# A plain weight unit split in two parts, in a fused two-block transformer kernel

## The chip, the cores and the metric

The kernel runs on one core of one Trainium2 chip. The metric is the device time of one execution in microseconds; the median of three runs of the kernel before is 2380.12 us (2380.11 to 2380.45). Every time below is from those runs or from one profiled execution.

## The reference, cut to what matters

Two transformer blocks follow each other on x of 1024 tokens by 1024 channels. The first has an HGRN2 mixer, the second a mixer of convolution and retention; both end in a squared-ReLU MLP with 4096 hidden channels, all float32:

```python
def _squared_relu_mlp(h, w1, w2):
    a = jax.nn.relu(h @ w1)
    return (a * a) @ w2

def sq_relu_mlp(u, w_up, w_down):
    hdn = jax.nn.relu(u @ w_up)
    return (hdn * hdn) @ w_down

x = x + _squared_relu_mlp(_rmsnorm(x, norm_mlp[layer]), mlp_w1[layer], mlp_w2[layer])   # block 1
h = h + sq_relu_mlp(rms_norm(h, norm2_g), w_up, w_down)                                 # block 2
```

The change touches only the product `h @ w1` (and `u @ w_up`) of the two MLPs, and there only the order in which weights are prepared.

## The kernel before, in words

**Products.** Each float32 operand is used as a high part (a cast to `fp32r`) and a low part (the float32 value minus the high part). A product of a 128x128 weight tile with 512 tokens is three matmuls: high by high, high weight by low operand, low weight by high operand (in `upper`, L905, L906 and L907; in `wino`, L820, L821 and L822).

**Weights.** They arrive as units of 128 x 8 x 128 floats (512 KB) in `w_raw`, which has two slots. Even units use slot 0 and odd ones slot 1. SyncE loads the units in order (`load_units`, L398, the load is L395) and waits for `w_split` before a slot is loaded again: unit n is loaded once units 0 to n - 2 are split.

**The MLP.** Its up product makes two hidden tiles of 128 channels at a time, an up pair, of which there are 16 in each MLP. An up pair takes two units. The first, in slot 0, holds the first 512 input channels and is used in a Winograd form: seven products of quarter size (A11, S1, A12, S2, S4, S3, A22) against prepared sums of the operand. GpSimd, ScalarE and VectorE make its parts together (`split_pair`, L478, with `weight_sums` on VectorE and `weight_highs` on ScalarE). The second, in slot 1, is the plain unit: input channels 512 to 1023 for both hidden tiles. Its slices 0 to 3 belong to the first hidden tile and slices 4 to 7 to the second. GpSimd alone splits it, in `split_unit` (L445): one cast of all 1024 columns (L450), and behind a wait for it four subtractions of 256 columns (L454), the last of which raises `w_split`.

**TensorE's order in an up pair** (`up_pair`, L911): A11, S1, A12, S2, S4, each of 6 matmuls, then the first plain block `upper(b_w, 0, 0)` with 12 matmuls, S3, the second plain block `upper(b_z, 1, 1)`, A22, and two more plain blocks. The first argument after the bank chooses the hidden tile, and so the half of the plain unit: 0 reads slices 0 to 3, 1 reads slices 4 to 7. Ahead of the first plain block stands

```python
pe.wait_ge(w_split, at(g, 8, u + 2))
```

which is true once the whole plain unit is split, and a second wait for `w_split` at u + 1 stands ahead of A22. Results of an up pair are taken from PSUM by VectorE (`finish_up`, L1546) and ScalarE (`copy`, L2234). A22 waits for `up_taken`, which VectorE raises once it has read what S3 left in the same bank; S3 waits for ScalarE's third copy of the pair.

**Groups.** Each MLP runs two up pairs, six groups, and two more up pairs. A group is an up pair in the near banks (b_w in `prod_ps`), four down pairs (`pairs`, L857), and an up pair in the far banks (b_w in `side_ps`). The first five groups are a hardware loop. A near pair follows directly on a far pair. In the near pair of a group VectorE also builds sums and low parts of hidden activations for the down pairs (`near_phase`, L1600: five instructions of 1024 columns at L1536 and L1532). In the near pair behind the last group it does not; the hidden tiles left are used in plain form.

**Who does what on GpSimd.** `split_mlp` (L497) goes through the units in order: for an up pair `split_pair` and then `split_unit`, which waits until the unit has landed and until TensorE is done with the previous unit in slot 1.

Of the kernel before, what the change touches and what calls it, by code (L numbers as in the profile page):

```python
# [37 lines left out]
ALU = mybir.AluOpType  # L38
ACT = mybir.ActivationFunctionType
F32 = mybir.dt.float32  # L40
# [15 lines left out]
WINO_GROUPS = 6  # L56
# [10 lines left out]
MLP_PLAIN_DOWN = WINO + (WINO + PAIRS) * WINO_GROUPS + 4  # L67
# [5 lines left out]
UP_PAIRS = FF // (2 * P)  # L73
MLP_PAIRS = UP_PAIRS + PAIRS * WINO_GROUPS
# [83 lines left out]
def at(g, step, first):  # L158

    return g * step + first  # L160


def build(nc, stream, x_t, gains, conv_w, lower_bound, head_rows, head_scalars, rope, ident_in, ones_in, masks_in, out_t):
    with ExitStack() as ctx:
# [15 lines left out]
        def sem(name):  # L180
            return ctx.enter_context(nc.semaphore(name))
# [8 lines left out]
        w_raw = place("w_raw", [P, 2, KT, P])  # L190
        w_hi = place("w_hi", [P, 2, KT, P], F32R)
        at_w_lo = room(8 * KB)
        w_lo = place("w_lo", [P, 2, KT, P], F32R, at=at_w_lo)
# [90 lines left out]
        w_landed = [sem("w_landed0"), sem("w_landed1")]  # L284
# [5 lines left out]
        high_begun = sem("high_begun")  # L290
        high_made = sem("high_made")
        w_split = sem("w_split")
        tiles_used = sem("tiles_used")
        prod = sem("prod")
# [9 lines left out]
        w_sum = sem("w_sum")  # L304
        w_high = sem("w_high")
        w_parts = sem("w_parts")
        down_prod = sem("down_prod")
        down_taken = sem("down_taken")
        up_prod = sem("up_prod")
# [134 lines left out]
        def _(pool):  # L444
            def split_unit(u, slot):  # L445
                pool.wait_ge(w_landed[slot], (u - slot) * 8 + 16)
                if not (isinstance(u, int) and u < 2):
                    pool.wait_ge(prod, u * 2 - 2)
                pool.sem_inc(high_begun, 1)
                nc.gpsimd.tensor_copy(w_hi[:, slot], w_raw[:, slot]).then_inc(high_made, 1)  # L450
                pool.wait_ge(high_made, u + 1)
                for part in range(4):
                    ks = slice(part * KT // 4, (part + 1) * KT // 4)
                    low = nc.gpsimd.tensor_tensor(w_lo[:, slot, ks], w_raw[:, slot, ks],  # L454
                                                  w_hi[:, slot, ks].bitcast(F32), ALU.subtract)
                low.then_inc(w_split, 1)
# [21 lines left out]
            def split_pair(u, slot, q):  # L478
# [15 lines left out]
                low(a22_lo[slot][:], w_raw[:, slot, 6:8], more_hi[slot][:, 4:6], 4).then_inc(w_split, 1)  # L494
                pool.sem_inc(high_made, 1)

            def split_mlp(u0, index):  # L497

                def up_pair(u, q):
                    split_pair(u, 0, q)  # L500
                    split_unit(u + 1, 1)

                def group(g, q):
                    up_pair(at(g, 8, u0 + 4), at(g, 6, q + 2))
                    for p in range(PAIRS):
                        split_pair(at(g, 8, u0 + 6 + p), p % 2, at(g, 6, q + 3 + p))
                    up_pair(at(g, 8, u0 + 10), at(g, 6, q + 7))

                q = index * MLP_PAIRS
                up_pair(u0, q)  # L510
                up_pair(u0 + 2, q + 1)
                with pool.Fori(0, WINO_GROUPS - 1) as g:
                    group(g, q)
                group(WINO_GROUPS - 1, q)
                up_pair(u0 + MLP_PLAIN_DOWN - 4, q + MLP_PAIRS - 2)
                up_pair(u0 + MLP_PLAIN_DOWN - 2, q + MLP_PAIRS - 1)

            for u in range(2):
                for part in range(4):
                    ks = slice(part * KT // 4, (part + 1) * KT // 4)  # L520
# [5 lines left out]
                    else:  # L526
                        high.then_inc(high_made, 1)
                        pool.wait_ge(high_made, u + 1)
                    low = nc.gpsimd.tensor_tensor(w_lo[:, u, ks], w_raw[:, u, ks], w_hi[:, u, ks].bitcast(F32),
                                                  ALU.subtract)  # L530
# [15 lines left out]
        def _(pe):  # L546
# [281 lines left out]
            def mlp(u0, index, before, h_before, t_norm, count, roots, left=0):  # L828


                first_group, first_up, first_pair = index * WINO_GROUPS, index * UP_PAIRS, index * MLP_PAIRS

                def parts(g, q, part):
                    pe.wait_ge(w_parts, at(g, 24, 4 * (first_pair + q) + part))

                def free(g, p, name):
                    pe.wait_ge(down_taken, at(g, PAIR_PRODUCTS, first_group * PAIR_PRODUCTS + pair_index(p, name)))
# [55 lines left out]
                def upper(into, i, half, first, start, mid=None):  # L893

                    act = slice(half * HALF, (half + 1) * HALF)
                    for kk in range(KT - X_WINO):
                        k = X_WINO + kk
                        if start:
                            pe.wait_ge(u_ready, before + 2 * k + half + 1)
                        if kk == 2 and mid is not None:  # L900
                            mid()
                        w_h, w_l = w_hi[:, 1, 4 * i + kk], w_lo[:, 1, 4 * i + kk]
                        a_h, a_l = hi[0][:, k, act], lo[0][:, k, act]
                        more = not (first and kk == 0)
                        nc.tensor.matmul(into, w_h, a_h, start=not more, stop=False, skip_group_check=not first)  # L905
                        nc.tensor.matmul(into, w_h, a_l, start=False, stop=False, skip_group_check=not first)  # L906
                        mm = nc.tensor.matmul(into, w_l, a_h, start=False, stop=kk == KT - X_WINO - 1,  # L907
                                              skip_group_check=not first)
                    return mm

                def up_pair(g, r, q, u, into, start=False, behind_down=False, hooks=(None, None, None, None), last=False):  # L911

                    b_u, b_v, b_w, b_z = into
                    u += u0
                    after_p5, after_p3, after_p7, in_last = hooks

                    def copied(n):
                        pe.wait_ge(up_copied, at(g, 8, 4 * (first_up + r) + n))

                    parts(g, q, 1)  # L920
                    if start:
                        pe.wait_ge(u_ready, before + 2 * X_WINO)
                    pe.wait_ge(evac, at(g, 16, 2 * u - 2 if start else 2 * u - 4))
                    if behind_down:
                        free(g, PAIRS - 2, "P4")
                    wino(b_u, 0, A11, x_op[B11], True).then_inc(up_prod, 1)
                    parts(g, q, 2)
                    pe.wait_ge(evac, at(g, 16, 2 * u - 2))
                    wino(b_v, 0, S1, x_op[T1], True).then_inc(up_prod, 1)
                    if after_p5 is not None:  # L930
                        after_p5()
                    if start:
                        pe.wait_ge(evac, 2 * u - 1)
                    wino(b_w, 0, A12, x_op[B21], True)
                    parts(g, q, 3)
                    copied(1)
                    wino(b_u, 0, S2, x_op[T2], False).then_inc(up_prod, 1)
                    parts(g, q, 4)
                    copied(2)
                    wino(b_v, 0, S4, x_op[B22], False)  # L940
                    if after_p3 is not None:
                        after_p3()
                    pe.wait_ge(w_split, at(g, 8, u + 2))
                    upper(b_w, 0, 0, False, start).then_inc(up_prod, 1)
                    copied(3)
                    wino(b_u, 0, S3, x_op[T3], False).then_inc(up_prod, 1)
                    if after_p7 is not None:
                        after_p7()
                    if start:
                        pe.wait_ge(evac, 2 * u)  # L950
                    upper(b_z, 1, 1, True, start).then_inc(up_prod, 1)
                    pe.wait_ge(w_split, at(g, 8, u + 1))
                    pe.wait_ge(up_taken, at(g, 2, first_up + r + 1))
                    wino(b_u, 0, A22, x_op[T4], False).then_inc(prod, 2)
                    if last:
                        upper(b_u, 1, 0, False, start).then_inc(up_prod, 1)
                        upper(b_v, 0, 1, False, start, in_last).then_inc(prod, 2)
                    else:
                        upper(b_v, 0, 1, False, start).then_inc(up_prod, 1)
                        upper(b_u, 1, 0, False, start, in_last).then_inc(prod, 2)  # L960

                def group(g):
                    up_pair(g, 2, 2, 4, near_banks, hooks=(None, None, None, lambda: first(g, 0)))
                    pairs(g)
                    up_pair(g, 3, 7, 10, far_banks, behind_down=True,
                            hooks=(lambda: fourth(g, PAIRS - 1), None, None, None))
# [10 lines left out]
                u = u0 + MLP_PLAIN_DOWN  # L977
# [109 lines left out]
            for j in range(CONV_TILES):  # L1087
                for part in range(3):
                    u = U_CONV + 3 * j + part
# [1430 lines left out]
```

## Time and profile before

| what | value |
|---|---|
| median of the timed runs | 2380.12 us |
| profiled execution | 2377.08 us |
| its span, first to last instruction | 2374.5 us |
| TensorE busy | 2331.4 us, 98% |
| VectorE busy | 1499.9 us, 63% |
| GpSimd busy | 1068.4 us, 45% |
| ScalarE busy | 724.5 us, 31% |
| mean granted TensorE clock | 0.997 of full speed |

In the rows PE is TensorE's matmul, DVE is VectorE, ACT is ScalarE, POOL is GpSimd and SP is SyncE. Matmuls overlap: each of 512 columns is listed with 0.39 us, while the next begins about 0.23 us after it. The distance between the starts of two matmuls is therefore what counts. A wait is listed under the instruction that waited, with what released it.

### The profile page before, as it was taken

How to read it: one execution, taken by the hardware profiler on the slowest of the kernel's cores; microseconds unless marked ns; L12 is line 12 of the kernel's file. 1: busy time of each engine (PE TensorE's matmuls, PEld its weight loads, DVE VectorE, ACT ScalarE, POOL GpSimd, SP SyncE). 2: the span in 40 equal slices, each digit the busy share in tenths (PEclk: the TensorE clock that was granted, in tenths of full speed). 3: DMA queues.
4: the chain of work that ended last, by engine and by line, in shares of the span. 5: the costliest groups of instructions: out<-in, count | busy, mean ns of one | idle time of the engine just before them, and what ended most of it. 6: DMA issues, size and time to landing. Idle time of an engine off the chain costs nothing.

```text
span 2374.5 us, 31836 instructions
## 1 busy us (share of the span) xinstructions
PE 2331.4 (98%) x11044; PEld 1939.2 (82%) x11044; DVE 1499.9 (63%) x2090; ACT 724.5 (31%) x1175; POOL 1068.4 (45%) x1186
## 2 busy tenths in 40 slices
PE   9999999999999999999999999999999999999998
PEld 6888888888787778778888888888877877787886
DVE  6666667756567666765566656454666676667434
ACT  4233333423433432333330002003343333323311
POOL 4322232345456555645443324453554565555432
PEclk9999999999999999999999999999999999999999
DMA  4110101031111111111111111111111111111112
GB/s 151 36 36 27 36 26 36 27 107 62 45 54 54 51 54 53 53 44 54 54 52 64 36 45 36 54 36 54 38 54 52 53 53 44 60 55 45 49 58 80
DMA packets 37526, 123.33 MB, mean 52 GB/s; under 512 B 4800, under 2 KB 5952, under 8 KB 37440
## 3 DMA queue, kind: packets, MB, share of 16 engines
q1 hardware_dynamic: 36432, 120.54, 16.0%
q10 hardware_dynamic: 1008, 1.62, 0.2%
q8 instruction: 57, 0.93, 0.2%
q14 instruction: 29, 0.24, 0.0%
HBM read 117.95 MB, written 4.19 MB: 51 GB/s over the span
## 4 chain that ended last, share of the span: by engine, by line
PE 82%; POOL 7%; issue 7%; DVE 2%; DVEq 1%; DMA 0%; SPq 0%; ACT 0%; POOLq 0%
PE prod_ps L563 13%; PE prod_ps L565 13%; PE prod_ps L564 13%; PE side_ps L822 4%; PE side_ps L821 4%; PE side_ps L820 4%; POOL w_lo L454 4%; PE prod_ps L822 4%; PE prod_ps L821 4%; PE prod_ps L820 4%; PE prod_ps L905 3%; PE prod_ps L906 3%; PE prod_ps L907 3%; PE side_ps L700 2%; PE side_ps L616 2%
## 5 line engine op out<-in xcount | busy, mean ns | idle before, releaser
L563 PE MATMUL prod_ps<-operand_hi,w_hi 128*128 128x512 f32 x1464 | 584.0, 399 | 2.9 <-DVE hgrn_v_t L1150 1.6
L565 PE MATMUL prod_ps<-operand_hi,w_lo 128*128 128x512 f32 x1464 | 572.6, 391 | 0.0
L564 PE MATMUL prod_ps<-operand_lo,w_hi 128*128 128x512 f32 x1464 | 571.4, 390 | 0.0
L454 POOL TENSOR_TENSOR w_lo<-w_raw,w_hi 128x256 fp32r<-128x256 f32 x472 | 470.5, 1027 | 9.4
L450 POOL CAST w_hi<-w_raw 128x1024 fp32r<-128x1024 f32 x118 | 125.9, 1067 | 733.8 <-PE prod_ps L565 680.2
L484 POOL TENSOR_TENSOR w_lo<-w_raw,w_hi 128x256 fp32r<-128x256 f32 x160 | 144.0, 918 | 454.6 <-ACT w_hi L2172 454.6
L563 PEld LDWEIGHTS prod_ps<-operand_hi,w_hi 128*128 128x128 f32 x1464 | 275.9, 188 | 61.1 <-issue 3.3
L565 PEld LDWEIGHTS prod_ps<-operand_hi,w_lo 128*128 128x128 f32 x1464 | 275.5, 188 | 59.1
L564 PEld LDWEIGHTS prod_ps<-operand_lo,w_hi 128*128 128x128 f32 x1464 | 276.1, 189 | 53.4
L905 PE MATMUL prod_ps<-operand_hi,w_hi 128*128 128x512 f32 x384 | 151.7, 395 | 22.5 <-POOL w_lo L454 22.5
L906 PE MATMUL prod_ps<-operand_lo,w_hi 128*128 128x512 f32 x384 | 150.5, 392 | 0.0
L907 PE MATMUL prod_ps<-operand_hi,w_lo 128*128 128x512 f32 x384 | 150.2, 391 | 0.0
L484 POOL TENSOR_TENSOR w_lo<-w_s,w_hi 128x256 fp32r<-128x256 f32 x160 | 118.1, 748 | 41.8 <-ACT w_more_hi L2176 24.6
L1540 DVE TENSOR_TENSOR x_res<-side_ps,x_res 128x512 f32<-128x512 f32 x168 | 113.1, 684 | 32.3 <-PE side_ps L822 30.4
L484 POOL TENSOR_TENSOR w_s_lo<-w_s,w_more_hi 128x256 fp32r<-128x256 f32 x160 | 129.7, 831 | 0.0
L1540 DVE TENSOR_TENSOR x_res<-prod_ps,x_res 128x512 f32<-128x512 f32 x120 | 82.4, 687 | 70.9 <-PE prod_ps L822 69.7
L1532 DVE TENSOR_TENSOR wino_lo<-wino,wino_hi 128x1024 fp32r<-128x1024 f32 x72 | 99.7, 1397 | 17.9 <-ACT wino_hi L2228 15.9
L905 PEld LDWEIGHTS prod_ps<-operand_hi,w_hi 128*128 128x128 f32 x384 | 72.5, 189 | 42.7 <-POOL w_lo L454 27.7
L1266 DVE TENSOR_TENSOR hgrn_kq<-hgrn_kq,hgrn_decay 128x1024 f32<-128x1024 f32 x48 | 60.6, 1262 | 51.5 <-PE side_ps L700 50.2
L907 PEld LDWEIGHTS prod_ps<-operand_hi,w_lo 128*128 128x128 f32 x384 | 72.5, 189 | 15.3
L906 PEld LDWEIGHTS prod_ps<-operand_lo,w_hi 128*128 128x128 f32 x384 | 72.4, 189 | 15.0
L2172 ACT ACTIVATE w_hi<-w_raw 128x512 fp32r<-128x512 f32 x80 | 49.9, 624 | 112.1 <-PE side_ps L822 58.0
(304 smaller groups left out, 4655.2 us busy)
## 6 DMA issues: line engine op xcount, KB each, us to landing
w_raw<-stream SPq DMA_DIRECT2D x202, 512.0 KB, 3.5
x_in<-x_t SPq DMA_DIRECT2D x16, 256.0 KB, 5.6
x_res<-x_t SPq DMA_DIRECT2D x8, 512.0 KB, 4.4
out_t<-x_res SPq DMA_DIRECT2D x16, 256.0 KB, 2.1
w_raw<-stream SPq DMA_DIRECT2D x8, 128.0 KB, 4.8
masks_f<-masks SPq DMA_DIRECT2D x1, 896.0 KB, 7.4
ret_rows<-head_rows ACTq DMA_DIRECT2D x1, 512.0 KB, 3.7
ret_cos<-rope ACTq DMA_DIRECT2D x1, 512.0 KB, 4.6
```

Source lines behind the costliest of these rows:

```text
L454: low = nc.gpsimd.tensor_tensor(w_lo[:, slot, ks], w_raw[:, slot, ks], w_hi[:, slot, ks].bitcast(F32), ALU.subtract)
L484: return nc.gpsimd.tensor_tensor(dst, src, high.bitcast(F32), ALU.subtract)
L563: nc.tensor.matmul(into, w_h, a_h, start=(k == 0), stop=False)
L564: nc.tensor.matmul(into, w_h, a_l, start=False, stop=False)
L565: last = nc.tensor.matmul(into, w_l, a_h, start=False, stop=(k == KT - 1))
L820: nc.tensor.matmul(into, w_h, a_h, start=first and kk == 0, stop=False, skip_group_check=not first)
L821: nc.tensor.matmul(into, w_h, a_l, start=False, stop=False, skip_group_check=not first)
L822: mm = nc.tensor.matmul(into, w_l, a_h, start=False, stop=kk == 1, skip_group_check=not first)
L905: nc.tensor.matmul(into, w_h, a_h, start=not more, stop=False, skip_group_check=not first)
L906: nc.tensor.matmul(into, w_h, a_l, start=False, stop=False, skip_group_check=not first)
L907: mm = nc.tensor.matmul(into, w_l, a_h, start=False, stop=kk == KT - X_WINO - 1, skip_group_check=not first)
L1540: nc.vector.tensor_tensor(x_res[:, m, tokens(half)], src, x_res[:, m, tokens(half)], ALU.add).then_inc(down_taken, 1)
```

## The change

GpSimd splits the plain unit of an up pair in two parts: a cast of slices 0 to 3, a wait for it, two subtractions that raise a new semaphore `upper_split`; then a cast of slices 4 to 7, a wait, two subtractions that raise `w_split`. TensorE's first plain block waits for `upper_split`, its second one for `w_split` of the plain unit, and the wait ahead of A22 is gone. Both new values are counted by up pair (r), 16 in each MLP. Everything outside `split_mlp` still uses `split_unit`.

```diff
--- before.py
+++ after.py
@@ -304,6 +304,8 @@
         w_sum = sem("w_sum")
         w_high = sem("w_high")
         w_parts = sem("w_parts")
+        upper_high = sem("upper_high")
+        upper_split = sem("upper_split")
         down_prod = sem("down_prod")
         down_taken = sem("down_taken")
         up_prod = sem("up_prod")
@@ -494,26 +496,44 @@
                 low(a22_lo[slot][:], w_raw[:, slot, 6:8], more_hi[slot][:, 4:6], 4).then_inc(w_split, 1)
                 pool.sem_inc(high_made, 1)
 
+            def split_upper(u, r):
+
+                pool.wait_ge(w_landed[1], u * 8 + 8)
+                pool.wait_ge(prod, u * 2 - 2)
+                pool.sem_inc(high_begun, 1)
+                nc.gpsimd.tensor_copy(w_hi[:, 1, 0:4], w_raw[:, 1, 0:4]).then_inc(upper_high, 1)
+                pool.wait_ge(upper_high, r + 1)
+                for ks in (slice(0, 2), slice(2, 4)):
+                    low = nc.gpsimd.tensor_tensor(w_lo[:, 1, ks], w_raw[:, 1, ks], w_hi[:, 1, ks].bitcast(F32),
+                                                  ALU.subtract)
+                low.then_inc(upper_split, 1)
+                nc.gpsimd.tensor_copy(w_hi[:, 1, 4:8], w_raw[:, 1, 4:8]).then_inc(high_made, 1)
+                pool.wait_ge(high_made, u + 1)
+                for ks in (slice(4, 6), slice(6, 8)):
+                    low = nc.gpsimd.tensor_tensor(w_lo[:, 1, ks], w_raw[:, 1, ks], w_hi[:, 1, ks].bitcast(F32),
+                                                  ALU.subtract)
+                low.then_inc(w_split, 1)
+
             def split_mlp(u0, index):
 
-                def up_pair(u, q):
+                def up_pair(u, q, r):
                     split_pair(u, 0, q)
-                    split_unit(u + 1, 1)
-
-                def group(g, q):
-                    up_pair(at(g, 8, u0 + 4), at(g, 6, q + 2))
+                    split_upper(u + 1, r)
+
+                def group(g, q, r):
+                    up_pair(at(g, 8, u0 + 4), at(g, 6, q + 2), at(g, 2, r + 2))
                     for p in range(PAIRS):
                         split_pair(at(g, 8, u0 + 6 + p), p % 2, at(g, 6, q + 3 + p))
-                    up_pair(at(g, 8, u0 + 10), at(g, 6, q + 7))
-
-                q = index * MLP_PAIRS
-                up_pair(u0, q)
-                up_pair(u0 + 2, q + 1)
+                    up_pair(at(g, 8, u0 + 10), at(g, 6, q + 7), at(g, 2, r + 3))
+
+                q, r = index * MLP_PAIRS, index * UP_PAIRS
+                up_pair(u0, q, r)
+                up_pair(u0 + 2, q + 1, r + 1)
                 with pool.Fori(0, WINO_GROUPS - 1) as g:
-                    group(g, q)
-                group(WINO_GROUPS - 1, q)
-                up_pair(u0 + MLP_PLAIN_DOWN - 4, q + MLP_PAIRS - 2)
-                up_pair(u0 + MLP_PLAIN_DOWN - 2, q + MLP_PAIRS - 1)
+                    group(g, q, r)
+                group(WINO_GROUPS - 1, q, r)
+                up_pair(u0 + MLP_PLAIN_DOWN - 4, q + MLP_PAIRS - 2, r + UP_PAIRS - 2)
+                up_pair(u0 + MLP_PLAIN_DOWN - 2, q + MLP_PAIRS - 1, r + UP_PAIRS - 1)
 
             for u in range(2):
                 for part in range(4):
@@ -940,7 +960,7 @@
                     wino(b_v, 0, S4, x_op[B22], False)
                     if after_p3 is not None:
                         after_p3()
-                    pe.wait_ge(w_split, at(g, 8, u + 2))
+                    pe.wait_ge(upper_split, at(g, 2, first_up + r + 1))
                     upper(b_w, 0, 0, False, start).then_inc(up_prod, 1)
                     copied(3)
                     wino(b_u, 0, S3, x_op[T3], False).then_inc(up_prod, 1)
@@ -948,8 +968,8 @@
                         after_p7()
                     if start:
                         pe.wait_ge(evac, 2 * u)
+                    pe.wait_ge(w_split, at(g, 8, u + 2))
                     upper(b_z, 1, 1, True, start).then_inc(up_prod, 1)
-                    pe.wait_ge(w_split, at(g, 8, u + 1))
                     pe.wait_ge(up_taken, at(g, 2, first_up + r + 1))
                     wino(b_u, 0, A22, x_op[T4], False).then_inc(prod, 2)
                     if last:
```

## Rows read from the trace of the kernel before

**Rows 1.** The page's part 1: busy time (share of the span) and instructions

```profile
PE 2331.4 (98%) x11044; PEld 1939.2 (82%) x11044; DVE 1499.9 (63%) x2090; ACT 724.5 (31%) x1175; POOL 1068.4 (45%) x1186
```

**Rows 2.** The page's part 4: the chain that ended last, by engine

```profile
PE 82%; POOL 7%; issue 7%; DVE 2%; DVEq 1%; DMA 0%; SPq 0%; ACT 0%; POOLq 0%
```

**Rows 3.** The waits, whole span: us in total, times, longest

```profile
PE prod_ps L905 <- POOL w_lo L454: 22.5, 12, 1.9
```

**Rows 4.** Timeline of PE, near pair: start, duration, engine, line, operation

```profile
719.39 0.40 PE L822 MATMUL prod_ps<-xop_hi,w_s_lo 128*128 128x512 f32 x1
721.65 0.50 PE L905 MATMUL prod_ps<-operand_hi,w_hi 128*128 128x512 f32 x1 [1.87 <-POOL w_lo L454]
724.51 0.39 PE L820 MATMUL prod_ps<-xop_hi,w_more_hi 128*128 128x512 f32 x1
728.62 0.39 PE L820 MATMUL prod_ps<-xop_hi,w_more_hi 128*128 128x512 f32 x1
```

**Rows 5.** Timeline of PE, the far pair before it

```profile
698.73 0.40 PE L822 MATMUL prod_ps<-xop_hi,w_s_lo 128*128 128x512 f32 x1
701.70 0.39 PE L820 MATMUL side_ps<-xop_hi,w_more_hi 128*128 128x512 f32 x1
```

**Rows 6.** Timelines of POOL: near pair, far pair, near pair after the last group

```profile
713.86 1.04 POOL L450 CAST w_hi<-w_raw 128x1024 fp32r<-128x1024 f32 x1
714.98 3.27 POOL L454 TENSOR_TENSOR w_lo<-w_raw,w_hi 128x256 fp32r<-128x256 f32 x2
714.98 6.62 POOL L454 TENSOR_TENSOR w_lo<-w_raw,w_hi 128x256 fp32r<-128x256 f32 x4
...
692.23 2.83 POOL L454 TENSOR_TENSOR w_lo<-w_raw,w_hi 128x256 fp32r<-128x256 f32 x4
...
1124.00 2.82 POOL L454 TENSOR_TENSOR w_lo<-w_raw,w_hi 128x256 fp32r<-128x256 f32 x4
```

**Rows 7.** Timeline of PE, near pair after the last group

```profile
1127.47 0.39 PE L905 MATMUL prod_ps<-operand_hi,w_hi 128*128 128x512 f32 x1
```

**Rows 8.** Timelines of DVE: near pair, then after the last group

```profile
714.47 3.19 DVE L1536 TENSOR_TENSOR wino<-wino,stage 128x1024 f32<-128x1024 f32 x2
719.51 3.18 DVE L1532 TENSOR_TENSOR wino_lo<-wino,wino_hi 128x1024 fp32r<-128x1024 f32 x2 [0.17 <-issue]
724.71 0.69 DVE L1567 TENSOR_TENSOR stage<-prod_ps,stage 128x512 f32<-128x512 f32 x1 [2.02 <-PE prod_ps L907]
726.09 0.69 DVE L1573 TENSOR_TENSOR stage<-prod_ps,stage 128x512 f32<-128x512 f32 x1
726.70 1.22 DVE L1532 TENSOR_TENSOR wino_lo<-wino,wino_hi 128x1024 fp32r<-128x1024 f32 x1
728.82 0.69 DVE L1577 TENSOR_TENSOR stage<-prod_ps,stage 128x512 f32<-128x512 f32 x1 [0.91 <-PE prod_ps L907]
740.68 0.42 DVE L1448 TENSOR_TENSOR w_s<-w_raw 128x256 f32<-128x256 f32 x1
...
1130.40 0.69 DVE L1567 TENSOR_TENSOR plain_raw<-prod_ps,plain_raw 128x512 f32<-128x512 f32 x1 [8.16 <-PE prod_ps L907]
```

**Rows 9.** POOL by line (ns min/median/max), and a cast of 128 columns

```profile
L450 POOL CAST w_hi<-w_raw x118: 1029/1041/1561, 27.2 to 2337.8; 128x1024 fp32r<-128x1024 f32 x118
L454 POOL TENSOR_TENSOR w_lo<-w_raw,w_hi x472: 716/742/1749, 28.6 to 2341.3; 128x256 fp32r<-128x256 f32 x158
520.44 0.29 POOL L468 CAST w_hi<-w_raw 128x128 fp32r<-128x128 f32 x1 [7.62 <-PE prod_ps L565]
```

**Rows 10.** Timeline of PE, second up pair of an MLP

```profile
616.67 0.40 PE L822 MATMUL prod_ps<-xop_hi,w_s_lo 128*128 128x512 f32 x1
620.20 0.39 PE L820 MATMUL side_ps<-xop_hi,w_more_hi 128*128 128x512 f32 x1
```

**Rows 11.** Timeline of ACT, near pair

```profile
719.80 0.58 ACT L2236 ACTIVATE stage<-prod_ps 128x512 f32<-128x512 f32 x1
```

**Rows 12.** The page's part 6: a load's size, median us to landing

```profile
w_raw<-stream SPq DMA_DIRECT2D x202, 512.0 KB, 3.5
```

## The prediction

> **What bounds the kernel now.** I read the busy times first: TensorE is busy for 98% of the span and no other engine for more than 63% [rows 1], so a change that touches GpSimd alone can only pay where TensorE stands still. The chain of waits says the same with one addition: 82% of it is TensorE and 7% is GpSimd [rows 2]. The list of TensorE's waits names the place. It waits for `w_lo` of L454 in front of L905, 12 times, 22.5 us in total and 1.9 us at most [rows 3]; L905 is `upper`, the plain blocks of an up pair, and L454 the low part of the plain unit's weights.
>
> The timeline of TensorE shows one such wait. The last matmul of S4 starts at 719.39, the first plain matmul at 721.65, the first of S3 at 724.51 [rows 4]: 5.12 us for 13 starts. In the far pair just before, the same 13 starts run from 698.73 to 701.70, 2.97 us [rows 5], or 0.228 us each. So a stall costs 2.15 us, a little more than the 1.9 us listed, because the first matmul behind a wait also starts up more slowly.
>
> Why is GpSimd late there and nowhere else? In that near pair its cast begins at 713.86 and takes 1.04 us, and the four subtractions end at 714.98 + 6.62 = 721.60, right ahead of TensorE's 721.65. In the far pair the same four took 2.83 us, in the near pair after the last group 2.82 us, ending at 1126.82 [rows 6]; there TensorE's first plain matmul starts at 1127.47 without any wait [rows 7]. The difference is VectorE: beside the slow subtractions it runs five subtractions or sums of 1024 columns from 714.47 to 722.69 (two, one, and two), about 1.59 us each, where one with GpSimd idle takes 1.22 [rows 8]. In the near pair after the last group it has nothing between those times; its next instruction comes at 1130.40 after 8.16 us of waiting [rows 8]. So the two engines slow each other: one GpSimd subtraction goes from 0.74 us (median) to about 1.65 us [rows 6, 9].
>
> How many places: the wait on `prod_ps` comes 12 times [rows 3]: the near pairs of the six groups in both MLPs, 2 x 6. In the second up pair of each MLP (2 places, with the bank in `side_ps`) 616.67 to 620.20 is 3.53 us for the same 13 starts [rows 10], 0.56 us too long.
>
> **The change part by part.** All times below are in the clock of the near pair above.
>
> 1. The first cast is halved. There is no 512-column cast in the trace. One of 128 columns takes 0.29 us, one of 1024 takes 1.04 (median) [rows 9]; on the straight line between them 512 columns take 0.29 + 3 x 0.107 = 0.61 us. It ends at 714.47. The gap from cast to subtraction was 0.08 us, so the first subtraction starts at 714.55 instead of 714.98. The first two took 3.27 us [rows 6] under VectorE's load; at that price the new signal `upper_split` stands at 717.8, and if the early start wins nothing, at 718.25, where the second one ended before.
>
> 2. TensorE arrives at the first plain block at 719.39 + 0.23 = 719.62. The margin is 1.4 to 1.8 us, so the wait of 2.15 us goes altogether.
>
> 3. The second cast now stands inside the contended stretch. Alone it takes 0.61 us. Contended, I bound it by a turn of a contended subtraction, 1.65 us; the longest cast in the trace, with twice the columns, took 1.56 [rows 9]. From below the bound is the 128-column cast, 0.29. I take 0.9, nearer to the row for it alone, as a contended 1024-column cast lost only 0.52 us against its median. Then 0.08 us for its own signal, and the last two subtractions at their old price, 721.60 - 718.25 = 3.35 us. `w_split` of the unit comes at 717.8 + 0.9 + 0.08 + 3.35 = 722.1, between 721.5 and 723.4 with both ends, the latter also with the late start.
>
> 4. That signal is now wanted by the second plain block, behind 12 matmuls of the first and 6 of S3: 719.62 + 18 x 0.228 = 723.7. The margin is 1.6 us at my value, 0.3 at the bad end. I cost this wait at nothing. If the cover were gone, each 0.1 us would cost 1.2 us over 12 pairs.
>
> 5. What is queued behind these waits on TensorE: S3 and everything after. TensorE has as many waits per pair as before, since the one ahead of A22 is dropped; I take their cost as zero. S3 wants ScalarE's copy of `b_u`, which ends at 719.80 + 0.58 = 720.4 [rows 11], against 722.35, when S3 would now start. A22 wants VectorE's `up_taken`. VectorE's low parts end at 722.69 [rows 8]; the first block's result is there at about 722.7 too (now 724.71, minus 2.15 = 722.56). Its next step, up to the addition behind S3, waits for TensorE again, as do the ones after it (0.91 us of idle time before 728.82). `up_taken` comes with the end of the addition of 726.09, at 726.78, 1.8 us ahead of A22 at 728.62 [rows 4, 8], and stays 1.4 us ahead even if VectorE is delayed by one more GpSimd turn, 1.59 - 1.22 = 0.4 us. So the pair and the pairs behind it move forward with TensorE.
>
> 6. SP's loads. `w_split` of the plain unit frees the buffer for the next load of slot 1. It moves from 721.6 to about 722.1 and the load lands in 3.5 us (median) [rows 12], near 725.6; the next slot-1 unit is first read by VectorE at 740.68 [rows 8]. Hidden by some 14 us. The other slot's signal, load and split are untouched.
>
> 7. The 20 other up pairs get 0.61 + 0.61 - 1.04 + 0.08 = 0.26 us more GpSimd work. In the far pair GpSimd is done at 695.06 and TensorE wants it after 698.73: hidden. Added register and wait instructions on GpSimd sit in the idle time that it has before nearly every unit.
>
> 8. The second up pair of each MLP wins its 0.56 us: the first half needs only half of the work there.
>
> The sum: 12 x 2.15 + 2 x 0.56 = 25.8 + 1.1 = 26.9 us. The profiled execution took 2377.08 us (span 2374.5); it would take 2350.2. The median of the timed runs is 2380.12, 3.04 above it, and the stalls are no likelier to be shorter there, so I subtract the same: 2353.2.
>
> **A rule that speaks against it.** The rows show that a pair of contended instructions (one VectorE, one GpSimd) takes 1.59 to 1.65 us [rows 6, 8], less than 1.22 + 0.74 = 1.96, the sum of the two alone. The Trainium skill, page "SBUF — State Buffer", section "SBUF: two separate sides", says that the port pair which VectorE and GpSimd share is an exclusive lock held for the whole instruction, taken also by a VectorE instruction with two SBUF inputs, and that the loser fully blocks. By that rule the second cast pays a whole turn of its own. The trace agrees that they hinder each other and not that nothing overlaps. What full blocking would make is rival A.
>
> **The rivals.**
> A. Full turns. Each GpSimd instruction in the stretch waits out a VectorE one, 1.96 us per turn. First signal: 714.55 + 3.92 = 718.5, still in time. Then cast and two subtractions, 5.88 us, end at 724.4: 0.7 us late for the second block, 12 x 0.7 = 8.4 us given back, 2361.6. For it: the order of issue is new. Against it: turns of 1.65 us now, and VectorE has only five such instructions, the last ending near 722.7, after which GpSimd is undisturbed. 7%.
> B. VectorE becomes the bound. It is busy without a gap from 714.47 to 722.69, and a longer stretch by the extra turn, or too little slack in the pairs behind, turns into a wait for `up_taken` or a freed bank. Losing 1.0 us per group gives 12 us back, 2365.2. Against it: the idle times of 2.02 and 0.91 us behind [rows 8]. 3%.
> C. It does not do what it says: TensorE stands as long as now, ahead of the second block, or at another wait of the pair for 2.15 us. 2380. It would need the second half at 725.9. 3%.
> D. Slower. The same place, beyond C: the second half has 723.7 - 717.8 = 5.9 us; from 8.0 us on it costs more than the stall did, and each 0.1 us beyond that costs 1.2 us over the 12 near pairs. At 8.6 us the kernel takes 2387. That asks for three instructions at 2.9 us each, against a longest subtraction of 1.749 and a longest cast of 1.561 [rows 9]. 3%.
>
> **How the numbers follow.** My forecast has 84% and its own range is 2351.5 to 2356: some tenths per pair from step 3 and the small starts. Rival A, the next likely, is partly inside the wider range up to 2359, which stands for a mild form of it (0.5 us per pair, 6 us in all). Below, nothing but the stalls can be won, so it ends at 2351.5. This kernel's measurement tells about 0.2%, 4.8 us. Faster by more than that: forecast, A and B, 94%. Within it: C, 3%. Slower: D, 3%.
>
> **What would show it.** In the changed profile the 12 waits of L905's successor on `w_lo` are gone, those on `side_ps` too, and no wait of comparable size stands at the second block or ahead of A22. The 13 starts around the first block take 2.97 us in the near pair. GpSimd shows two casts of 512 columns per up pair, the second between 0.6 and 1.65 us in near pairs. VectorE's step from the low parts to the first addition has no gap of 2.02 us. I am wrong if TensorE's idle time on GpSimd comes back behind S3 (A, D), or if idle time on VectorE appears (B).

## The result, and the profile after

The changed kernel takes 2347.59 us (median of 4 runs, 2347.34 to 2348.69), the one before, beside it, 2380.11 us. The ratio is 0.9864, its 95% interval 0.9847 to 0.9881. I had forecast 2353.2 with a range down to 2351.5: the direction was right, the gain was 32.5 us instead of 26.9, and the time lies 3.9 us below the range. The profiled execution took 2347.34 us, its span 2344.1, so 30.4 us less span than before.

The page of the changed kernel, the busy times and the chain, as [rows 1, 2]:

```profile
PE 2322.2 (99%) x11044; PEld 1939.3 (83%) x11044; DVE 1493.2 (64%) x2090; ACT 724.5 (31%) x1175; POOL 1084.9 (46%) x1218
PE 96%; DVE 2%; DVEq 1%; issue 0%; DMA 0%; SPq 0%; ACT 0%
```

GpSimd has left the chain that ended last; TensorE holds 96% of it instead of 82%. The list of TensorE's waits has no line on L925 (the old L905) any more, against [rows 3]; the longest that are left (us in total, times, longest) stand elsewhere:

```profile
PE prod_ps L583 <- DVE operand_lo L1183: 2.8, 4, 1.3
PE side_ps L660 <- DVEq L1941: 2.4, 1, 2.4
PE side_ps L720 <- DVE hgrn_scores L1308: 2.2, 1, 2.2
```

The same near pair as in [rows 4], TensorE's timeline (start, duration, engine, line, operation); the first line is the last matmul of A12, the second the last of S4:

```profile
714.27 0.39 PE L842 MATMUL prod_ps<-xop_hi,w_lo 128*128 128x512 f32 x1
717.00 0.40 PE L842 MATMUL prod_ps<-xop_hi,w_s_lo 128*128 128x512 f32 x1
717.24 0.39 PE L925 MATMUL prod_ps<-operand_hi,w_hi 128*128 128x512 f32 x1
719.97 0.39 PE L840 MATMUL prod_ps<-xop_hi,w_more_hi 128*128 128x512 f32 x1
721.35 0.39 PE L925 MATMUL prod_ps<-operand_hi,w_hi 128*128 128x512 f32 x1
```

From the last matmul of S4 to the first of S3 it is 2.97 us, as in the far pair [rows 5], and not 5.12. The second plain block starts at 721.35 without a wait. GpSimd beside it (compare [rows 6]):

```profile
711.66 0.61 POOL L504 CAST w_hi<-w_raw 128x512 fp32r<-128x512 f32 x1
712.35 3.41 POOL L507 TENSOR_TENSOR w_lo<-w_raw,w_hi 128x256 fp32r<-128x256 f32 x2
715.71 1.61 POOL L510 CAST w_hi<-w_raw 128x512 fp32r<-128x512 f32 x1
717.40 3.29 POOL L513 TENSOR_TENSOR w_lo<-w_raw,w_hi 128x256 fp32r<-128x256 f32 x2
```

The first signal comes at 715.76, 1.5 us before TensorE's 717.24, the second at 720.69, 0.66 us before 721.35. VectorE (compare [rows 8]) goes from its low parts straight to the first addition, without the 2.02 us of waiting:

```profile
712.27 2.90 DVE L1556 TENSOR_TENSOR wino<-wino,stage 128x1024 f32<-128x1024 f32 x2
717.02 3.07 DVE L1552 TENSOR_TENSOR wino_lo<-wino,wino_hi 128x1024 fp32r<-128x1024 f32 x2 [0.17 <-issue]
720.17 0.69 DVE L1587 TENSOR_TENSOR stage<-prod_ps,stage 128x512 f32<-128x512 f32 x1
```

**Where the 30.4 us of span went.** I laid TensorE's matmuls of the two traces beside each other and looked where the distance between their starts changes.

| place | before | changed | us in all |
|---|---|---|---|
| last matmul of S4 to the first of S3, 12 near pairs | 5.10 to 5.17 | 2.97 | 26.0 |
| the same, half clock behind one wait (2074.99) | 1.6 more | none | 1.6 |
| last matmul of A12 to the last of S4, 12 near pairs | 2.93 (2.83 and 2.85 in the first of each MLP) | 2.73 | 2.2 |
| last matmul of S4 to the first of S3, two second pairs | 3.53 | 2.97 | 1.1 |
| ahead of all these places (3201st matmul) | 606.9 | 607.5 | -0.6 |
| behind the last matmul | 9.0 | 8.8 | 0.2 |

The rows add up to the 30.4 us but for rounding. So the waits that I had priced gave 27.1 us against my 26.9, and the rest came from two things that I had not priced.

**The wait at S2.** It stands in the list of waits of the weight loads (PEld), which I had not read beside the list of the matmuls. The kernel before, its list of waits (us in total, times, longest):

```profile
PEld prod_ps L820 <- ACT stage L2236: 3.0, 10, 0.3
PEld prod_ps L820 <- issue: 0.6, 2, 0.3
```

The last matmul of A12, the weight load that waited, and ScalarE's copy, from the timelines of the near pair:

```profile
716.46 0.39 PE L822 MATMUL prod_ps<-xop_hi,w_lo 128*128 128x512 f32 x1
...
716.75 0.19 PEld L820 LDWEIGHTS prod_ps<-xop_hi,w_hi 128*128 128x128 f32 x1 [0.32 <-ACT stage L2236]
...
716.09 1.09 ACT L2236 ACTIVATE stage<-prod_ps 128x512 f32<-128x512 f32 x2 [0.88 <-DVE wino L1536]
```

Ten waits on ScalarE's copy and two filed under "issue", 3.6 us, one for each near pair of the groups. The load for the matmul of 716.46 starts at 716.24, ahead of it, so the matmuls lose less than the load waits: from 716.46 to the last of S4 at 719.39 [rows 4] it is 2.93 us, in the changed kernel 2.73 (714.27 to 717.00), 0.2 us a pair and 2.2 in all. S2 waits for `copied(1)`, and the copy waits for VectorE's first sum (L1536). After the change the copy starts at 713.61, 1.95 us after GpSimd's cast instead of 2.23, and both lines are gone from the list. Its timeline:

```profile
713.61 1.09 ACT L2256 ACTIVATE stage<-prod_ps 128x512 f32<-128x512 f32 x2 [0.58 <-DVE wino L1556]
```

VectorE's first sum ran beside the end of GpSimd's cast of 1024 columns (713.86 to 714.90); a cast of 512 is over when it starts, and the first two sums take 2.90 us instead of 3.19.

**The half clock.** Behind the wait that ends at 2074.99 the matmuls start 0.43 us apart instead of 0.23: TensorE's lower level, 1.2 GHz instead of 2.4. Eight such intervals cost 1.6 us. The kernel before, TensorE's timeline:

```profile
2074.99 0.63 PE L905 MATMUL prod_ps<-operand_hi,w_hi 128*128 128x512 f32 x1 [1.88 <-POOL w_lo L454]
2075.42 0.63 PE L906 MATMUL prod_ps<-operand_lo,w_hi 128*128 128x512 f32 x1
2078.74 0.39 PE L905 MATMUL prod_ps<-operand_hi,w_hi 128*128 128x512 f32 x1
```

And two stretches of it: length, TensorE's busy time, the granted clock as a share, the share and rate of DMA:

```profile
2074.00:2079.00 5.00, 4.01 (x11) 0.66 0.35 105
2088.00:2093.00 5.00, 5.00 (x24) 1.00 0.00 0
```

The changed kernel has no such stretch in its up pairs.

### The profile page after: what moved, and what is told of

It reads as the page before. It is cut to its first block, busy times and chain, and to the rows that moved or that the text cites. A ratio compares the mean times of both kernels' runs of the same rounds, so it can differ in the third digit from the quotient of the medians.

```text
span 2344.1 us, 31876 instructions
## 1 busy us (share of the span) xinstructions
PE 2322.2 (99%) x11044; PEld 1939.3 (83%) x11044; DVE 1493.2 (64%) x2090; ACT 724.5 (31%) x1175; POOL 1084.9 (46%) x1218
## 4 chain that ended last, share of the span: by engine, by line
PE 96%; DVE 2%; DVEq 1%; issue 0%; DMA 0%; SPq 0%; ACT 0%
PE prod_ps L583 13%; PE prod_ps L585 13%; PE prod_ps L584 13%; PE prod_ps L842 6%; PE prod_ps L841 6%; PE prod_ps L840 6%; PE side_ps L842 5%; PE side_ps L841 5%; PE side_ps L840 5%; PE prod_ps L926 4%; PE prod_ps L925 4%; PE prod_ps L927 4%; PE side_ps L720 2%; PE side_ps L636 2%; PE side_ps L642 1%; PE side_ps L926 1%
## 5 line engine op out<-in xcount | busy, mean ns | idle before, releaser
L452 POOL CAST w_hi<-w_raw 128x1024 fp32r<-128x1024 f32 x86 | 92.4, 1074 | 701.3 <-PE prod_ps L585 680.4
L486 POOL TENSOR_TENSOR w_lo<-w_raw,w_hi 128x256 fp32r<-128x256 f32 x160 | 143.9, 918 | 405.8 <-ACT w_hi L2192 405.8
L456 POOL TENSOR_TENSOR w_lo<-w_raw,w_hi 128x256 fp32r<-128x256 f32 x344 | 327.3, 981 | 6.9
L925 PE MATMUL prod_ps<-operand_hi,w_hi 128*128 128x512 f32 x384 | 149.9, 390 | 0.0
L925 PEld LDWEIGHTS prod_ps<-operand_hi,w_hi 128*128 128x128 f32 x384 | 72.2, 188 | 15.1
```

The lines of the kernel that those rows point to most:

```text
L486: return nc.gpsimd.tensor_tensor(dst, src, high.bitcast(F32), ALU.subtract)
```

## The experiments

Theory after the result: (1) the waits at the plain block, (2) the wait at S2, won by the shorter first cast, (3) stretches at half clock that the 2 us of idle time brought on. Rivals: that (2) and (3) are chance or come from another part of the edit (the wait dropped ahead of A22), and that GpSimd was late for another reason than VectorE. All runs:

| kernel | median us | runs | spans us | granted clock |
|---|---|---|---|---|
| before, beside the others | 2380.3 to 2382.0 | 43 | 2375.1 to 2380.9 | 0.994 to 0.997 |
| before again | 2379.87 | 11 | 2374.0 to 2380.0 | 0.994 to 0.997 |
| changed | 2347.59 | 4 | 2344.0 to 2346.2 | 0.996 to 0.998 |
| changed again | 2347.85 | 4 | 2343.6 to 2345.8 | 0.997 to 0.998 |
| split alone | 2414.96 | 5 | 2399.7 to 2412.8 | 0.984 to 0.992 |
| one cast | 2349.97 | 4 | 2346.8 to 2348.3 | 0.997 to 0.998 |
| A22 wait dropped | 2381.41 | 10 | 2376.6 to 2379.9 | 0.994 to 0.997 |
| sums left out | 2347.81 | 4 | 2345.3 to 2347.4 | 0.997 to 0.998 |
| second cast in two | 2346.48 | 4 | 2343.8 to 2345.3 | 0.997 to 0.998 |
| second part longer | 2359.13 | 4 | 2356.2 to 2357.8 | 0.997 to 0.998 |
| stall filled | 2377.55 | 11 | 2373.2 to 2377.2 | 0.995 to 0.998 |
| longer stall filled | 2391.02 | 5 | 2387.0 to 2390.1 | 0.996 to 0.998 |

### The two kernels once more

> The kernel before, unchanged, for its own run-to-run spread. Forecast theory (the 32.5 us are the stalls' 26.9 plus a second wait that went, plus slow-clock stretches behind stalls): spans of single runs differ from each other in steps of about 1.7 us, and a longer span comes with a lower mean granted clock; the median is 2380.1, some 2 to 3 us above the profiled 2377.08, because most runs have two or three such stretches against the one seen. Rival (the 3 us between profile and timed runs lie outside the span, in the launch): the clock of all runs is 0.997 and the spans are within 0.3 us of 2374.5.

> The changed kernel unchanged, beside the others of this call. Clock theory (a stall of 2 us in front of a plain block makes the chip grant half the clock for some matmuls behind it, in some of the places and runs; no stall, no such stretch): spans of all runs within 2343.8 to 2346.5, clock 0.996 to 0.998, while the kernel before spreads from 2374 to 2381 at 0.994 to 0.997. Rival (the kernel before is more scattered for another reason): the same scatter here.

The ratio is 0.9994 (0.9985 to 1.0003) for the first and 0.9856 (0.9839 to 0.9872) for the second. The kernel before scatters over 6 us of span, and its longer spans have the lower clock (2374.0 at 0.997, 2380.0 at 0.994). The changed kernel scatters over 2.6 us. Part of the scatter has nothing to do with the change: in the twelve traces TensorE's 3201st matmul, ahead of all the places above, starts anywhere between 606.6 and 608.7 us, and 0 to 15 matmuls of the first 60 us start 0.43 us apart. The floors, 2374.0 and 2343.6, are 30.4 apart, the medians 32 to 34. The profiled run of the kernel before lay near its floor, with an early start of that matmul (606.9) and one half-clock stretch. The 3 us between it and the median, which I had carried over as a constant, were span and not launch: a run takes some 2.5 us more than its span at the floor (2376.63 against 2374.0) as in the middle (2379.87 against 2377.4).

### The split without the earlier start

```diff
-                    pe.wait_ge(upper_split, at(g, 2, first_up + r + 1))
+                    pe.wait_ge(w_split, at(g, 8, u + 2))
                     upper(b_w, 0, 0, False, start).then_inc(up_prod, 1)
...
-                    pe.wait_ge(w_split, at(g, 8, u + 2))
                     upper(b_z, 1, 1, True, start).then_inc(up_prod, 1)
```

> GpSimd splits in two parts as in the changed kernel, TensorE waits for the whole unit as before. Forecast theory with a contended second cast of a full turn (GpSimd takes 9.03 us from its first cast to the end of the unit instead of 7.74): each near pair is 1.3 us longer than before, 12 x 1.3 = 15.5, the second pairs 0.3 each: 2396 us. Rival (the second cast took 1.6 us only because TensorE went on undelayed; the split itself costs its 0.26 us): 2380.1 + 12 x 0.26 = 2383 us. Second rival (the shorter first cast helps by itself through ScalarE's earlier copy): 2377 us.

2414.96 us, ratio 1.0135 (1.0119 to 1.0150), 19 us above the highest expectation. The waits are as long as forecast for a full turn of the second cast (15.6 us more than before), and TensorE pays for them twice. The trace is of the fastest of the five runs, 2403.06 us. Its list of waits:

```profile
PE prod_ps L925 <- POOL w_lo L513: 38.1, 12, 3.3
```

Its timeline in one near pair:

```profile
725.26 0.50 PE L925 MATMUL prod_ps<-operand_hi,w_hi 128*128 128x512 f32 x1 [3.31 <-POOL w_lo L513]
726.25 0.63 PE L925 MATMUL prod_ps<-operand_hi,w_hi 128*128 128x512 f32 x1
```

And the granted clock of that stretch and of a later one:

```profile
725.00:730.00 5.00, 4.74 (x14) 0.66 0.36 105
740.00:745.00 5.00, 5.00 (x24) 1.00 0.19 35
```

The trace has half-clock stretches behind 8 of its 12 waits of up to 3.3 us, of 5 to 12 matmuls each, some 12 us in all; the kernel before, with waits of 1.9 us, had one. The middle run took 12 us more than this one at a mean clock of 0.986 instead of 0.992; it has no trace. So the split by itself loses 33 us, although the wait at S2 is gone here too: the gain needs TensorE's earlier start on the first half.

### One cast, the signal after two subtractions

```diff
-                nc.gpsimd.tensor_copy(w_hi[:, 1, 0:4], w_raw[:, 1, 0:4]).then_inc(upper_high, 1)
-                pool.wait_ge(upper_high, r + 1)
+                nc.gpsimd.tensor_copy(w_hi[:, 1], w_raw[:, 1]).then_inc(high_made, 1)
+                pool.wait_ge(high_made, u + 1)
...
                 low.then_inc(upper_split, 1)
-                nc.gpsimd.tensor_copy(w_hi[:, 1, 4:8], w_raw[:, 1, 4:8]).then_inc(high_made, 1)
-                pool.wait_ge(high_made, u + 1)
```

> One cast of the whole plain unit as before, then two subtractions that raise upper_split, then two that raise w_split; TensorE waits as in the changed kernel. Theory A (0.27 us per near pair were won because the halved first cast lets VectorE's sums, and so ScalarE's first copy, come earlier): that wait at S2 is back, 12 x 0.27 = 3.3 us, 2350.9 us; GpSimd needs about 7.7 us for the unit and the first signal comes 18.25 - 13.86 = 4.4 us after its start, in time. Theory B (that part came from somewhere else in the change, such as the wait dropped ahead of A22): 2347.6 us.

2349.97 us, 2.1 to 2.4 above the two medians of the changed kernel, and no run of one reaches into the runs of the other. Theory A asked for 3.3 at my 0.27 us a pair; at the 0.2 that the matmuls show it is 2.2. Theory B asked for nothing. The wait is back in the weight loads, with the count and size that it had before the change, in its list of waits:

```profile
PEld prod_ps L838 <- ACT stage L2254: 3.0, 10, 0.3
PEld prod_ps L838 <- issue: 0.6, 2, 0.3
```

VectorE's two sums take 3.19 us again (timeline):

```profile
713.27 3.19 DVE L1554 TENSOR_TENSOR wino<-wino,stage 128x1024 f32<-128x1024 f32 x2
```

That ties the wait at S2 to the length of the first cast: beside VectorE's sums, every traced kernel with a cast of 1024 columns there has the wait, and every one with a cast of 512 does not. The medians differ by 0.1%, which alone would be thin; the trace agrees with them, since the last matmul of A12 to the last of S4 takes 34.9 us in its 12 near pairs and 32.8 in the changed kernel's. It also shows where the main gain comes from: with one cast of full width and TensorE's earlier start, all but these 2.1 to 2.4 us of the gain are there.

### The wait ahead of A22

```diff
-                    pe.wait_ge(w_split, at(g, 8, u + 1))
                     pe.wait_ge(up_taken, at(g, 2, first_up + r + 1))
```

> The kernel before, only the wait for w_split ahead of A22 dropped. Theory A (it is always passed already and costs nothing): 2380 us, the same as the kernel before within 1.5 us. Theory B (part of the gain that I did not forecast came from this dropped wait): 2376 to 2378 us, and the wait of 0.27 us at S2 is smaller.

2381.41 us, ratio 0.9998 (0.9988 to 1.0007): nothing, as forecast in step 5. The wait at S2 is there as before (3.0 us, 10 times).

### VectorE's sums left out

```diff
-                    combine(T3, op_raw[B22][:], stage_b12)
+                    def zero(op):
+                        nc.vector.memset(op_raw[op][:], 0.0).then_inc(t_made, 1)
+
+                    zero(T3)
...
```

T2 and T4 are replaced in the same way. This kernel leaves the three sums out and so computes something else; it is for the time alone.

> The kernel before, with the three 1024-column sums that VectorE makes in a group's near pair (L1536) replaced by fills with zero, which read nothing; the sums are left out. Theory A (GpSimd is late in that pair only because VectorE's instructions with two operands in SBUF run beside it): its four subtractions take 2.8 to 3.5 us instead of 6.6, end before TensorE wants them, and the 2.15 us waits and the 0.27 us wait at S2 are gone: 2380 - 25.8 - 3.3 and about 2 to 3 for the clock: 2348 to 2351 us. Theory B (GpSimd is slow there for another cause: ScalarE, the load, its own queue): the subtractions stay near 6.6 us and the time at 2377 to 2380.

2347.81 us, ratio 0.9860 (0.9844 to 0.9877). GpSimd's four subtractions in the near pair, untouched, now take 2.84 us as in the far pair, and no wait is left at the plain block of the near pairs. Its timeline of GpSimd:

```profile
711.94 1.03 POOL L450 CAST w_hi<-w_raw 128x1024 fp32r<-128x1024 f32 x1
713.05 2.84 POOL L454 TENSOR_TENSOR w_lo<-w_raw,w_hi 128x256 fp32r<-128x256 f32 x4
```

VectorE's three fills of 1024 columns ran beside them (712.79 to 716.27) and did not slow them; its two low parts began at 716.44, when GpSimd was done at 715.89, and took 1.18 us each instead of 1.59. So VectorE's instructions with two operands beside it caused the old stall, and the change removes the wait without removing that cause.

### How much room the second half has

The second cast in two:

```diff
-                nc.gpsimd.tensor_copy(w_hi[:, 1, 4:8], w_raw[:, 1, 4:8]).then_inc(high_made, 1)
+                nc.gpsimd.tensor_copy(w_hi[:, 1, 4:6], w_raw[:, 1, 4:6])
+                nc.gpsimd.tensor_copy(w_hi[:, 1, 6:8], w_raw[:, 1, 6:8]).then_inc(high_made, 1)
```

> As the changed kernel, but the second cast is made in two of 256 columns: one GpSimd instruction more in the contended stretch. In the changed kernel the second half is ready 0.65 us before TensorE wants it. Theory A (a GpSimd instruction is slowed only as long as VectorE has one of its five 1024-column instructions to run; the sixth is free): the second half ends some 0.7 us later, 0 to 0.2 us late, 2347.6 to 2350. Theory B (each GpSimd instruction there costs a turn of 1.6 us): 0.95 us late, 12 x 0.95 = 11.4, 2359 us.

And the last two subtractions made twice:

```diff
-                for ks in (slice(4, 6), slice(6, 8)):
...
+                for n in range(2):
+                    if n:
+                        pool.drain()
+                    for ks in (slice(4, 6), slice(6, 8)):
...
```

> As the changed kernel, but GpSimd makes the last two subtractions of the plain unit twice before it raises w_split. In the changed kernel the second half is ready 0.65 us before TensorE wants it; two more subtractions of 0.72 us and a drain make it 0.8 to 0.9 us late. Theory A (the second block takes over as the bound, my rivals A and D, with the price of the delay plus 0.11 us for the slower first matmul): 12 x 0.95 = 11.4, about 2359 us, and a new wait at the second block, 12 times. Theory B (something behind absorbs it): 2348. Clock: if only stalls of 2 us and more bring slow stretches, the clock stays at 0.997 to 0.998; if any stall does, it falls to 0.995 and the time is 2361 or more.

2346.48 us for the first, no loss at all, and 2359.13 for the second. GpSimd in the first:

```profile
710.71 0.61 POOL L504 CAST w_hi<-w_raw 128x512 fp32r<-128x512 f32 x1
714.75 1.40 POOL L510 CAST w_hi<-w_raw 128x256 fp32r<-128x256 f32 x1
716.09 1.46 POOL L511 CAST w_hi<-w_raw 128x256 fp32r<-128x256 f32 x1
717.63 2.29 POOL L514 TENSOR_TENSOR w_lo<-w_raw,w_hi 128x256 fp32r<-128x256 f32 x2
```

Two casts of 256 columns take 1.40 and 1.46 us, each not much less than the 1.61 of one of 512; the two subtractions behind them take 2.29 us instead of 3.29. The unit needs 9.21 us from its first cast, against 9.03. Theory A holds: a GpSimd instruction there costs about a turn whatever its width, but only while VectorE has one of its five instructions left. In the second kernel the half is late. Its list of waits:

```profile
PE prod_ps L928 <- POOL w_lo L516: 8.0, 12, 0.8
```

TensorE's timeline in a near pair of it:

```profile
717.72 0.39 PE L928 MATMUL prod_ps<-operand_hi,w_hi 128*128 128x512 f32 x1
722.79 0.50 PE L928 MATMUL prod_ps<-operand_hi,w_hi 128*128 128x512 f32 x1 [0.80 <-POOL w_lo L516]
```

The two blocks start 5.07 us apart instead of 4.11, so 0.96 us late, and 12 x 0.96 = 11.5 us against 11.3 measured. The clock stays at 0.997 to 0.998, and the trace has no half-clock stretch behind any of these waits of 0.8 us.

### TensorE's idle time filled with matmuls

```diff
+                    if q == 2 and in_last is not None:
+                        for _ in range(9):
+                            nc.tensor.matmul(b_z, w_hi[:, 0, 0], x_op[B11][0][:, 0], start=True, stop=True)
                     pe.wait_ge(w_split, at(g, 8, u + 2))
```

On the kernel before, nine matmuls that nobody reads:

> The kernel before, with nine matmuls that nobody reads (into the bank b_z, 9 x 0.228 = 2.05 us) ahead of the wait for w_split in the 12 near pairs of the groups, so that TensorE works through most of its wait of 2.15 us. Clock theory (TensorE standing idle for 2 us is what brings the stretches at half clock behind it): no such stretch in these pairs, spans of all runs near the floor of the kernel before, 2373 to 2375, time 2375.5 to 2377.5, mean clock 0.997 to 0.998. Rival (the clock falls there for another reason, for instance the load on the chip at that point or chance): the same scatter as the kernel before, median 2380 to 2382 at 0.994 to 0.997.

On the split alone, fourteen:

> The kernel with the split alone (TensorE waits for the whole unit; it had waits of 3.3 us, eight stretches at half clock in its trace, and 2415 us), with fourteen matmuls that nobody reads (3.2 us) ahead of that wait in the 12 near pairs. Clock theory: its 2415 us are 2396 us of longer wait, as I expected there, and the rest is clock; filled, it takes 2393 to 2397 us at 0.997. Rival (the rest is another cost of the split): 2411 to 2415 us, with or without the stretches.

The first takes 2377.55 us, ratio 0.9987 (0.9978 to 0.9996), with a floor of 2373.2 and no half-clock stretch in the MLPs. That is 2.8 us less than the kernel before beside it and at the slow end of what I expected; the spans still scatter over 4 us. It is a small effect, and the longer waits are the stronger test. The second takes 2391.02 us, ratio 1.0042 (1.0028 to 1.0056), against 1.0135 without the useless work, and has none of the eight stretches. One near pair of it:

```profile
722.54 3.35 PE L965 MATMUL prod_ps<-xop_hi,w_hi 128*128 128x512 f32 x14
726.04 0.50 PE L925 MATMUL prod_ps<-operand_hi,w_hi 128*128 128x512 f32 x1 [0.15 <-POOL w_lo L513]
726.38 0.40 PE L926 MATMUL prod_ps<-operand_lo,w_hi 128*128 128x512 f32 x1
```

TensorE goes on at 0.23 us a matmul. GpSimd finishes no earlier (0.15 us of the wait is still there; its unit takes 9.02 us from its first cast, against 8.98 on the split alone), so the 24 us between the medians are clock (the middle runs: 0.986 and 0.997). The traces say the same for their two runs: from S4 to S3 the 12 near pairs take 77.7 us in all instead of 90.1. It came out 2 us under the expectation; I had left out there that the wait at S2 is gone, 2.2 us, and had started from a median that held half-clock time of its own. Which of the two made the difference is not shown. The idle time is shown to be the cause of the half clock.

## Why the prediction was wrong

The place, the count and the mechanism of the main gain held, and so did its size: the waits that I had priced gave 27.1 us against 26.9. Two steps failed. Step 5 put what hangs on VectorE and ScalarE at nothing, and the sum took the clock as fixed; both left out a gain, and I had closed the range on that side.

- **Step 1**: the halved cast takes 0.61 us, as worked out.
- **Step 2**: the first signal comes 4.10 us after the cast's start, 3.94 at my value. The margin is 1.5 us, within my 1.4 to 1.8, and the wait is gone in all 12 pairs.
- **Step 3**: the second cast takes 1.61 us, at my upper bound of 1.65 and not at 0.9. I went by a wider cast that had been disturbed once; here VectorE is at its 1024-column instructions beside all but 0.2 us of it. The half is ready 9.03 us after the first cast's start instead of 8.2.
- **Step 4**: so the margin was 0.66 us and not 1.6. It held, and the longer second part confirms the price behind it, 12 us for each us.
- **Step 5, the first that failed**: no new wait came and the dropped one is worth nothing, but I followed only what comes after the first block. `copied(1)`, ahead of S2, was already a wait of 0.3 us, listed under the weight loads alone, and it hung on VectorE's first sum, which ran beside the cast that is halved. I had priced the shorter cast for GpSimd and not for what runs beside it. It was worth 2.2 us by the traces, 2.1 to 2.4 by the medians. By itself it takes the forecast to 2351.0, just out of the range.
- **Steps 6 and 7**: no trace of either in the waits.
- **Step 8**: 0.56 us each, as forecast.
- **The sum, the second that failed**: "nothing but the stalls can be won" left out that the idle time also cost clock, one stretch of 1.6 us in the profiled run. The 3.04 us between the profiled run and the median, which I carried over as a constant, were not one: the changed kernel's median lies 0.25 above its profiled run. By my estimate a middle run of the kernel before has one or two stretches more than the profiled one, and the rest is the scatter at the kernel's start; how the 3 us divide is not shown. With 27.1 us from the waits, 2.2 from S2 and 1.6 to about 3.5 from the clock it would have been 31 to 33.
- **The rule and rival A**: the cast pays a turn of its own, of 1.61 us and not 1.96. By the rule that I had cited from the Trainium skill, page "SBUF — State Buffer", section "SBUF: two separate sides", the loser is blocked for the whole instruction; the runs agree that the width hardly counts (1.40 and 1.61 us for 256 and 512 columns) and not that a turn is the sum of both instructions. Rival A named the right place: 0.96 us more made it the bound. B, C and D did not come. The 84% stood for a range that the time missed; what came true is the 94% for a gain of more than 4.8 us.

No experiment points to a version that beats the changed kernel: its near pairs have no wait left, and the second cast in two, 1.1 us lower, is within the scatter.

## What to carry to other kernels

Let the consumer start on the first part before making a late producer faster, and leave the second part as much room as its most disturbed instruction takes. Read the waits of the weight loads beside those of the matmuls, and where an instruction gets shorter, ask which other engine it was slowing. Where TensorE stands idle again and again, count its clock too: here a wait of 3.3 us cost another 1 us on average behind it in the traced run, and 2 us by the medians.

## What the runs showed of the hardware that I had not expected

TensorE fell to the lower of its two levels behind 8 of 12 waits of 3.3 us, behind 1 to 3 of 12 waits of 1.9 us (in three traces), and behind none of 12 waits of 0.8 us. Each stretch lasted 5 to 12 matmuls. Matmuls that nobody reads, in the place of the idle time, kept it at the upper level and made a kernel 24 us faster.

A GpSimd instruction beside VectorE's 1024-column sums takes 1.4 to 1.7 us whether it casts 256 columns, casts 512 or subtracts 256; alone the cast of 512 takes 0.61 and the subtraction 0.74. Beside VectorE's fills of the same width it is not slowed.
